# Six buffers of high parts, low parts in place, and GpSimd for every sixth low part of the light items

## The reference

```
hid = silu(tokens @ w1) * (tokens @ w3)      # 1024 x 3584 each
y   = gate * (hid @ w2)                      # 3584 x 1024
```

## Time and profile before

| | us |
|---|---|
| median of three runs (2112.20 to 2115.09) | 2114.43 |
| the profiled execution | 2117.29 |
| its span, first to last instruction | 2115.2 |
| first item, about | 1155.2 to 1282.8 |
| light items | 1282.8 to 1627.3 (114.8, 114.9, 114.8) |
| full items | 1627.3 to 2104.7 (119.6, 119.5, 119.6, ...) |

### The profile page before, as it was taken

How to read it: one execution, slowest core, us unless ns; L and a number is a source line. 1 busy time by engine, 2 the same in 40 slices (tenths; PEclk the granted TensorE clock), 3 DMA queues, 4 the chain that set the end, 5 groups by cost and what they waited for, 6 DMA issues and landing times.

```text
span 2115.2 us, 32333 instructions
## 1 busy us (share of the span) xinstructions
PE 2045.8 (97%) x12532; PEld 1762.9 (83%) x12532; DVE 1607.6 (76%) x1966; ACT 1303.7 (62%) x1611; POOL 80.5 (4%) x58
## 2 busy tenths in 40 slices
PE   6999999999999999999999999999999999999998
PEld 6899999999999989999999785555556888888886
DVE  6667986558885765555644888898888888888897
ACT  2645553555553654334643678888887777777776
POOL 0000000000000300000000000000000000000010
PEclk6999999999999999999999999999999999999999
DMA  9975455565445434554529899999999999999991
GB/s 288 242 236 173 154 167 140 134 185 185 121 140 152 148 109 148 182 188 132 184 66 355 325 370 382 404 388 395 388 406 377 383 374 384 376 379 386 358 396 72
DMA packets 315525, 548.27 MB, mean 259 GB/s; under 512 B 68364, under 2 KB 208577, under 8 KB 315401
## 3 DMA queue, kind: packets, MB, share of 16 engines
q1 hardware_dynamic: 306384, 530.81, 71.8%
q0 software_dynamic: 3168, 11.54, 1.8%
q10 hardware_dynamic: 5848, 4.19, 0.7%
HBM read 539.14 MB, written 7.36 MB: 258 GB/s over the span
## 4 chain that ended last, share of the span: by engine, by line
PE 85%; DVE 10%; ACT 3%; issue 1%; ACTq 0%; DMA 0%; DVEq 0%
PE bank L742 22%; PE bank L744 22%; PE bank L743 22%; DVE w_lo L2902 6%; PE bank L689 2%; PE bank L895 2%; PE bank L1325 1%; PE bank L1431 1%; PE bank L702 1%; ACT w_hi L2099 1%; PE bank L1432 1%; PE bank L727 1%; PE bank L1451 1%; PE bank L878 1%; PE bank L864 1%
## 5 line engine op out<-in xcount | busy, mean ns | idle before, releaser
L2902 DVE TENSOR_TENSOR w_lo<-pool,w_hi 128x2048 fp32r<-128x2048 f32 x336 | 761.3, 2288 | 87.9 <-ACT w_hi L2099 86.5
L2099 ACT ACTIVATE w_hi<-pool 128x2048 fp32r<-128x2048 f32 x336 | 638.5, 1915 | 133.8 <-PE bank L744 114.5
L742 PE MATMUL bank<-h_upper,upper 128*128 128x256 f32 x1056 | 312.0, 295 | 3.6 <-DVE h_lo L2439 3.2
L743 PE MATMUL bank<-h_lo,upper 128*128 128x256 f32 x1056 | 299.6, 284 | 0.0
L744 PE MATMUL bank<-h_upper,ring_lo 128*128 128x256 f32 x1056 | 299.5, 284 | 0.0
L2340 DVE TENSOR_TENSOR ring_lo<-ring,upper 128x1024 fp32r<-128x1024 f32 x148 | 179.9, 1221 | 102.9 <-ACT upper L1617 102.4
L742 PE MATMUL bank<-w_hi,xe_hi 128*128 128x512 f32 x560 | 222.5, 397 | 4.5 <-DVE w_lo L2902 4.5
L2639 DVE TENSOR_TENSOR piece_lo<-ring,piece_hi 128x1024 fp32r<-128x1024 f32 x118 | 145.0, 1237 | 97.3 <-ACT piece_hi L1606 97.0
L744 PE MATMUL bank<-w_hi,xe_lo 128*128 128x512 f32 x560 | 218.9, 391 | 0.0
L743 PE MATMUL bank<-w_lo,xe_hi 128*128 128x512 f32 x560 | 218.7, 391 | 0.0
L742 PEld LDWEIGHTS bank<-h_upper,upper 128*128 128x128 f32 x1056 | 203.0, 192 | 6.4 <-issue 4.7
(11 more groups left out here) (454 smaller groups left out, 3682.6 us busy)
## 6 DMA issues: line engine op xcount, KB each, us to landing
pool<-in_od_exp_w SPq DMA_DIRECT2D x336, 1024.0 KB, 7.9
ring<-in_w_in SPq DMA_DIRECT2D x48, 1024.0 KB, 5.4
ring<-in_ev_ffn_w SPq DMA_DIRECT2D x33, 1024.0 KB, 5.3
ring<-in_w_ada SPq DMA_DIRECT2D x24, 1024.0 KB, 6.5
ring<-in_od_w_in SPq DMA_DIRECT2D x12, 1024.0 KB, 5.9
ring<-in_ev_w_in SPq DMA_DIRECT2D x10, 1024.0 KB, 5.3
ring<-in_w_in SPq DMA_DIRECT2D x32, 256.0 KB, 4.6
ring<-in_w_out SPq DMA_DIRECT2D x8, 1024.0 KB, 5.0
```

The costliest lines, as they stand in the source:

```text
L742: nc.tensor.matmul(b, left[0], right[0], start=first, stop=False, skip_group_check=True)
L743: nc.tensor.matmul(b, left[0], right[1], start=False, stop=False, skip_group_check=True)
L2099: nc.scalar.activation(w_hi[q % 3], ring_slot(q), ACT.Copy)\
L2902: V.tensor_tensor(w_lo[q % 3], ring_slot(q), w_hi[q % 3].bitcast(F32), ALU.subtract)\
```

## The change

Three `w_hi`/`w_lo` pairs become six `w_hi`, and the low part is written over the half tile in its ring slot (`low_slot`). So SP may load q + 14 only once the product of q is done. ACT may run six half tiles ahead of PE. `BEHIND` and `LOW_ROWS` are moved back by one to three half tiles, the folds of w1 behind the second half tile that follows, and the folds of w3 behind both half tiles of `down`. In the light items the low parts of q = 3, 9, 15, 21, 27, 33 and 39 are formed by GpSimd, from a list written out for the three items, with `add_rows` ahead of q = 9 and `gather_rows` ahead of q = 27; PE waits for them on a semaphore of their own, and DVE counts such a step together with its next low part. `item_tables` is cut in three and done behind q = 7, 9 and 11, and PE's transposes of the gates wait for the gates alone.

```
@@ -159,6 +159,8 @@
...
         oa_hi = sb("oa_hi", 4, S, dt=F32R, within=over)
+    with ExitStack() as over:
+        expert_lo = [sb(f"expert_lo{n}", EHALF, dt=F32R, within=over) for n in range(ERING)]
     pool = ctx.enter_context(nc.sbuf_tensor("pool", [P, POOL], F32))[:, :]
@@ -194,9 +196,10 @@
...
-    w_hi, w_lo = [None] * 3, [None] * 3
-    for i in (1, 2, 0):
-        w_hi[i], w_lo[i] = sb(f"w_hi{i}", EHALF, dt=F32R), sb(f"w_lo{i}", EHALF, dt=F32R)
+    HIS = 6
+    w_hi = [None] * HIS
+    for i in (2, 3, 4, 5, 0, 1):
+        w_hi[i] = sb(f"w_hi{i}", EHALF, dt=F32R)
     xe_hi, xe_lo = sb("xe_hi", KD, P, dt=F32R), sb("xe_lo", KD, P, dt=F32R)
@@ -620,12 +624,16 @@
...
-    BEHIND = {1: [("y", 0)], 3: [("own rows", 0)], 5: [("hid", 0)], 9: [("hT", 0)], 11: [("gateT", 0)],
-              13: [("hid", 1), ("hid", 2)], 14: [("pick", 0)], 15: [("hT", 1)], 19: [("hT", 2)], 20: [("rows", 0)],
-              23: [("hid", 3), ("hid", 4)], 27: [("hT", 3)], 31: [("hT", 4)], 35: [("hid", 5), ("hid", 6)],
-              37: [("hT", 5)], 39: [("hT", 6)], 40: [("xe", 0)], 41: [("xe", 1)]}
-
-    LOW_ROWS = {3: (1, 0), 5: (3, 0), 9: (1, 1), 13: (3, 1), 19: (1, 2), 23: (3, 2), 31: (1, 3), 35: (3, 3)}
+    def low_slot(q):
+        return expert_lo[(q + ERING_FIRST) % ERING]
+
+    BEHIND = {4: [("y", 0)], 5: [("own rows", 0)], 7: [("hid", 0)], 11: [("hT", 0)], 13: [("gateT", 0)],
+              15: [("hid", 1), ("hid", 2)], 16: [("pick", 0)], 17: [("hT", 1)], 21: [("hT", 2)], 22: [("rows", 0)],
+              25: [("hid", 3), ("hid", 4)], 29: [("hT", 3)], 33: [("hT", 4)], 37: [("hid", 5), ("hid", 6)],
+              38: [("hT", 5)], 40: [("hT", 6)], 41: [("xe", 0), ("xe", 1)]}
+
+    LOW_ROWS = {4: (1, 0), 6: (3, 0), 10: (1, 1), 14: (3, 1), 20: (1, 2), 24: (3, 2), 32: (1, 3), 36: (3, 3)}
+    POOL_LOWERS = range(3, NH, 6)
     FIRST, LIGHTS = -1 - LIGHT, range(-LIGHT, 0)
@@ -1409,8 +1417,11 @@
...
-                pe.wait_ge(item_vector, at(item_vector, i, "lo", q))
-                return [split(w[q % 3], a, EHALF // a) for w in (w_hi, w_lo)]
+                if light and q in POOL_LOWERS:
+                    pe.wait_ge(pool_lower, when(pool_lower, i, q))
+                else:
+                    pe.wait_ge(item_vector, at(item_vector, i, "lo", q))
+                return [split(w, a, EHALF // a) for w in (w_hi[q % HIS], low_slot(q))]
@@ -1452,7 +1463,7 @@
...
-            def down(blk, behind=lambda: None):
+            def down(blk):
                 pe.wait_ge(item_vector, at(item_vector, i, "hT", blk))
@@ -1467,8 +1478,6 @@
...
                     m.then_inc(item_products, tick(item_products, "half", q))
-                    if half == 0:
-                        behind()
@@ -1478,29 +1487,30 @@
...
                 list_rows().then_inc(psum_ready, wrote("own rows"))
-            up(3, 0, 0)
+            up(3, 0, 0, 1)
             fold(1, 0)
-            up(3, 0, 1)
             if first:
...
                         pe.wait_ge(tok_ready, when(tok_ready, "x", t, g))
-            up(1, 1, 0)
+            up(1, 1, 0, 1)
             fold(3, 0)
-            up(1, 1, 1, 2, 3)
+            up(1, 1, 2, 3)
             turn_hidden(0)
             up(3, 1, 0)
-            fold(1, 1)
             if first:
                 pe.wait_ge(route_ready, when(route_ready, "own rows"))
-                pe.wait_ge(route_ready, when(route_ready, "tables"))
+                pe.wait_ge(route_ready, when(route_ready, "gates"))
             for t in range(NT):
...
             m.then_inc(item_products, tick(item_products, "gateT"))
-            up(3, 1, 1, 2, 3)
+            up(3, 1, 1)
+            fold(1, 1)
+            up(3, 1, 2, 3)
             if not first:
                 pe.wait_ge(item_scalar, at(item_scalar, i, "y", 1))
-            down(0, lambda: fold(3, 1))
+            down(0)
+            fold(3, 1)
             turn_hidden(1)
@@ -1509,20 +1519,22 @@
...
             list_rows().then_inc(item_products, tick(item_products, "rows"))
-            up(3, 2, 0)
+            up(3, 2, 0, 1)
             fold(1, 2)
-            up(3, 2, 1, 2, 3)
-            down(1, lambda: fold(3, 2))
+            up(3, 2, 2, 3)
+            down(1)
+            fold(3, 2)
             down(2)
...
             turn_hidden(4)
-            up(3, 3, 0)
+            up(3, 3, 0, 1)
             fold(1, 3)
-            up(3, 3, 1, 2, 3)
-            down(3, lambda: fold(3, 3))
+            up(3, 3, 2, 3)
+            down(3)
+            fold(3, 3)
             wait_turned(4)
@@ -2096,15 +2108,15 @@
...
                 act.wait_ge(s, value)
-            nc.scalar.activation(w_hi[q % 3], ring_slot(q), ACT.Copy)\
+            nc.scalar.activation(w_hi[q % HIS], ring_slot(q), ACT.Copy)\
                 .then_inc(item_scalar, tick(item_scalar, "hi", q) + more)
...
             if k == 3:
-                piece_of_expert(FIRST, 0, (piece_ready, when(piece_ready, piece_no[("gg3",), 1])), freed_at[where["odout", 0]])
+                piece_of_expert(FIRST, 0, (piece_ready, when(piece_ready, piece_no[("gg3",), 1])))
             if k == 5:
-                piece_of_expert(FIRST, 1, freed_at[where["odout", 2]])
+                piece_of_expert(FIRST, 1, freed_at[where["odout", 0]])
@@ -2148,11 +2160,11 @@
...
             for q, (w, blk, half) in enumerate(halves):
-                if first and q == 2:
-                    piece_of_expert(i, q, freed_at[where["router",]], more=2)
-                elif q > 2 or not first:
-                    piece_of_expert(i, q, (item_products, at(item_products, i, "half", q - 3) if q >= 3 else
-                                           at(item_products, i, "half", q - 3 + NH, items=-1)))
+                if first and 2 <= q < HIS:
+                    piece_of_expert(i, q, freed_at[where[("odout", q - 1) if q < HIS - 1 else ("router",)]], more=2 * (q == HIS - 1))
+                elif q > 1 or not first:
+                    piece_of_expert(i, q, (item_products, at(item_products, i, "half", q - HIS) if q >= HIS else
+                                           at(item_products, i, "half", q - HIS + NH, items=-1)))
                 if first and q == 17:
@@ -2899,7 +2911,7 @@
...
             dve.wait_ge(item_scalar, at(item_scalar, i, "hi", q))
-            V.tensor_tensor(w_lo[q % 3], ring_slot(q), w_hi[q % 3].bitcast(F32), ALU.subtract)\
+            V.tensor_tensor(low_slot(q), ring_slot(q), w_hi[q % HIS].bitcast(F32), ALU.subtract)\
                 .then_inc(item_vector, tick(item_vector, "lo", q) + more)
@@ -2983,6 +2995,7 @@
...
             V.tensor_copy(item_expert[:, 0:NE].bitcast(I32), item_order)
+            yield
             link(V.tensor_tensor(ours, iota8.unsqueeze(1).broadcast_to(square), item_order.unsqueeze(2).broadcast_to(square),
@@ -3026,6 +3040,10 @@
...
             ticks.counts[("route_ready", "items")] = ticks.counts["route_ready"]
+            yield
+
+        tables = item_tables()
+
@@ -3052,10 +3070,12 @@
...
             for q, (w, blk, half) in enumerate(halves):
-                if q > 1 or not first:
-                    expert_lower(i, q)
-                if first and q == 4:
-                    item_tables()
+                if light and q in POOL_LOWERS:
+                    tick(item_vector, "lo", q)
+                elif q > 1 or not first:
+                    expert_lower(i, q, more=int(light and q - 1 in POOL_LOWERS))
+                if first and q in (7, 9, 11):
+                    next(tables)
                 for step, n in after(q):
@@ -3195,9 +3215,18 @@
...
         gather_rows(-1)
+        for i in range(LIGHT):
+            for q in POOL_LOWERS:
+                if q == POOL_LOWERS[1]:
+                    add_rows(i)
+                if q == POOL_LOWERS[4]:
+                    gather_rows(i)
+                pool_engine.wait_ge(item_scalar, at(item_scalar, i - LIGHT, "hi", q))
+                G.tensor_tensor(low_slot(q), ring_slot(q), w_hi[q % HIS].bitcast(F32), ALU.subtract)\
+                    .then_inc(pool_lower, tick(pool_lower, i - LIGHT, q))
         pool_engine.wait_ge(route_ready, when(route_ready, "items"))
         count = pool_engine.value_load(item_count[0:1, 0:1].bitcast(I32), min_val=NE, max_val=MAXI)
-        with pool_engine.Fori(0, count - 1) as i:
+        with pool_engine.Fori(LIGHT, count - 1) as i:
             add_rows(i)
@@ -3241,7 +3270,7 @@
...
         for q in range(NH - ERING):
-            sp.wait_ge(item_vector, at(item_vector, FIRST, "lo", q))
+            sp.wait_ge(item_products, at(item_products, FIRST, "half", q))
             load(0, q + ERING)
@@ -3251,22 +3280,22 @@
...
         for q in range(NH - ERING, NH):
-            sp.wait_ge(item_vector, at(item_vector, FIRST, "lo", q))
+            sp.wait_ge(item_products, at(item_products, FIRST, "half", q))
             load(following, q + ERING - NH)
...
-                sp.wait_ge(item_vector, at(item_vector, i, "lo", q, items=-LIGHT))
```

(6 more changed lines are left out.)

## The result

The changed kernel takes 2142.97 us (median of four runs, 2132.65 to 2147.24), against 2114.76 for the kernel before beside it: ratio 1.0129, interval 1.0092 to 1.0166. It is 1.3% slower, and outside the predicted range. The profiled execution is the shortest of the four, 2132.65, so it shows only 15.4 us of the loss (span 2130.6, against 2115.2).

What follows compares the result with a forecast made beforehand. PE was taken to bound full items, and nothing alone light items, with their mutual waits. 2117.29 - 6.0 (tables) + 4.1 (three light items) = 2115.4, less 2.9 for the profiled execution's excess over the median: 2112.5 us; range 2101 to 2121.

Steps and rivals of the forecast that it cites:

- Does it run beside DVE?: Low parts on GpSimd and DVE: they take turns by whole instructions; seven moved ones take 31.5 us of turns, not 15.5.
- A light item, step by step: Light item laid out from its product 0: 116.2 us against 114.9 before, 1.4 more in each of three, +4.1 in all.
- my list (9, 17, 21, 26, 33): Five places in a light item where GpSimd's turns were to take back the gain of six buffers.
- What six buffers bring: Light items: fewer waits on low parts, taken back by GpSimd's turns; together 1.4 us more an item.
- The DMA ... can't become less than 110.2: Light item's 114.9 us at 393 GB/s: 410 at best allows 110.2, except ring stock, 2.6 us once per half tile.
- The tables in three parts: First item: PE's 4.50 us hole and lower clock go, 6.2 us together; 0.2 comes back at low part 12; -6.0.
- Rival 4: First item: the tables' third part makes the hole again at product 12; gain about 2.5, sum 2116; chance 0.07.
- The price of an undisturbed low part, 4.5: GpSimd's low part: 4.5 us, twice the 2.26 us of a half-length `tensor_tensor` with two different operands.
- Rival 1: GpSimd's low part costs 3.8 us; light items 112.6, total 2101.7; chance 0.32 with what lies between it and the forecast.
- Full items at 0: Four full items: no change from 119.5 us, as every low part stays two or more half tiles ahead.
- rival 2: GpSimd's turn is dearer, 5.2 us at each of five places in a light item; total 2123.1; chance 0.20.
- Rival 3: No turns taken at this length: DVE's load falls to 87 us, light items to 110.2 or 109; total 2090.7; chance 0.05.

Runs made afterwards that it cites:

- after: The changed kernel as profiled, all parts of the change against the kernel before; its profiled execution took 2132.65 us, the median of four runs 2142.97.
- experiment 2: Changed kernel with the next item's gather issued behind GpSimd's low part of q = 27 instead of ahead of it; 2140.78 us, ratio 1.0123.
- experiment 5: Changed kernel with GpSimd forming only the low part of q = 27 in each light item, DVE the other 41; 2123.75 us, ratio 1.0054.
- experiment 6: Changed kernel with GpSimd forming only the low part of q = 28 in each light item, DVE all others; 2116.38 us, ratio 1.0018.
- experiment 1: Changed kernel with all low parts of the light items on DVE, none on GpSimd; 2085.54 us, ratio 0.9867.
- experiment 3: Changed kernel with low part 27 given back to DVE, GpSimd keeping 3, 9, 15, 21, 33 and 39; 2103.5 us, ratio 0.9953.
- Experiment 9: Changed kernel, but in light items DVE waits for GpSimd's low part 27 before forming its own 28; 2113.47 us, ratio 0.9996.
- experiment 8: Changed kernel with GpSimd's seven low parts an item replaced by a memset of the same size; 2084.34 us, ratio 0.9868.
- experiment 4: Kernel before with only the tables cut in three, behind q = 6, 8 and 10, and gate transposes waiting for gates alone; 2112.39 us, ratio 0.9995.
- experiment 10: Changed kernel with GpSimd's low parts at three other places in each light item, such as 3, 18, 30; 2111.73 us in one execution.

## Why the prediction was wrong

**The failed step is "Does it run beside DVE? ... So they take turns, whole instruction by whole instruction."** The first half held: the two didn't run at the same time. A low part of DVE that began while GpSimd had its turn ended 2.1 us after GpSimd's did (at q = 21 of after's first light item 1335.14 against 1333.00, recorded with 4.53). The second half assumed fair turns, one instruction each. With the next low part ready each time, DVE kept the turn, for 12 to 14 us in after's first light item and in every one of experiments 2, 5 and 6, and for nearly 7 in after's other two. That is 39 of the 57 us that GpSimd's work costs (experiments 1, 3). The rows I drew it from had only short queues: in the earlier trace rows DVE itself waited for high parts between its low parts (1.66 and 0.19), so GpSimd found gaps. I read a rule for a full queue from a stretch without one.

**"A light item, step by step" came out right for fair turns, in sum.** It gave 116.2, with product 27 not late. Experiment 9, where the turn at 27 is enforced, has 115.6 and 116.6 between gathers. In its second light item PE waited for GpSimd at 9, 21 and 33, as laid out (1.46, 1.87 and 1.90 us). At 26, where the layout had 1.9 us, it didn't wait, and a wait of 1.56 at product 2 wasn't in the layout, so part of the agreement is luck. In after the items lose another 3 to 10 us, at product 27, where my list (9, 17, 21, 26, 33) had 1.9 us for low part 26 and nothing for 27.

**What six buffers bring was never priced by itself.** It stood in the layout only as netted against GpSimd's turns (+1.4). By itself the rest of the change brings 28 us (experiment 1), 23 of it over the three light items. Had I laid out the item with all low parts on DVE, the comparison would have shown that every us of the gain was there without GpSimd, and the question would have been what GpSimd adds: with free relief, nothing (experiment 8).

**"The DMA ... can't become less than 110.2"** is undercut: 105.9. The stated exception, what the ring holds in advance, was priced at 2.6 a half tile once. The steady rate was a little higher (403 over a whole item), and the rest is stock: loads landing in 19.5 us tell that it runs low. An estimate from the stretches: 403 GB/s over 105.9 us are 42.7 MB, where 393 over 114.9 were 45.2, so an item took some 2.5 MB from the ring's stock, worth about 6 us at that rate. By this estimate a longer row of light items would not stay at 105.9; no run shows it.

**"The tables in three parts", -6.0, measured about -3.3** (first item, from its first product to the transposes of the next tokens, 111.5 against 114.8, the same in after and experiment 1). Product 12 was 1.35 us late, not 0.2, and the transposes of `turn_hidden(1)` 1.62, which I had counted in light items only:

```profile
1189.33 0.47 PE L750 MATMUL bank<-w_hi,hT_hi 128*128 128x512 f32 x1 [1.35 <-DVE expert_lo L2914]
...
1196.64 0.66 PE L1462 MATMUL bank<-ident,hid 128*128 128x128 f32 x4 [1.62 <-DVE hid L3089]
```

These are after's two waits of PE behind low parts and `hid` there. Rival 4 had named product 12. With three buffers, and the parts one half tile earlier, the longest wait is twice that, at product 11 (2.71, experiment 4).

**The price of an undisturbed low part, 4.5, was right:** 4.59 to 4.63. Rival 1's 3.8 is refuted.

**Full items at 0** held: 119.2 against 119.5, PE without a wait.

**The rivals.** The nearest in sign was rival 2, "GpSimd's turn is dearer", at 2123. Its mechanism, a dearer instruction at every place, isn't what happened: six of seven cost 4.6 to 6.3, and one cost 11 to 18. But one of its grounds was "turns lost to DVE", and that is what was lost, at one place. I had written that handing over costs nothing as an argument against it, and from one row. Rival 3 (no turns, 2090.7) came within 5.2 us of what the change gives without GpSimd's low parts (2085.5), by the wrong cause.

Why low part 27 took 11.3 us in the second and third item and 18.5 in the first, and 18.5 three times in experiment 2, can be read from the traces: in the 11.3 high part 30 came 0.52 us after low part 29 had ended, in the 18.5 it was ready 0.26 us or more before. A shift of under a us so decides over 7 us. The runs of after spread by 14.6 us, and the profiled one is the shortest; two items by 7.2 us more would be 14.4, but only that one has a trace, so that this is the spread's cause isn't shown. What stays open is why GpSimd gets the turn at q = 3 of two items though DVE's next low part is ready, and what 128x1 instructions have that lets them in (below).

## What to carry to other kernels

Before work is moved to a second engine that shares a path with a busy one, ask how long the busy one's queue of ready instructions is at that moment: the newcomer may be served only when that queue is empty. More buffers allow a longer queue; here six let six low parts go first, and GpSimd's low parts with fewer buffers were not run. Price each part of a change alone as well as in sum, since here a gain of 28 us stood beside a loss of 57 and was netted away on paper. And ask what the relieved engine was worth: when a third resource stands close behind, removing its work brings nothing.

## What the runs showed of the hardware

- Two-operand subtractions on DVE, each ready when the one before ends, can keep a GpSimd subtraction waiting for all of them: up to 18.8 us for a 4.6 us instruction, behind six of DVE's. Wherever it was passed over, 61 times in seven traces, DVE's next operand was ready (experiment 10). The Trainium skill (SBUF — State Buffer, "Who interferes with whom") says that issue order decides who blocks. Here the measurement differs: GpSimd's instruction began at 1342.99 and DVE's low parts at 1343.49 and later, and all six of these went first. When each engine asks for the ports isn't recorded, so the first of the six could be a matter of half a us; the last three began 7.4 us later and more.
- Tiny instructions of GpSimd (128x1) do get in, at the end of the one low part in progress: 2.17 us at 1335.86 of after, with the next low part following at once, instead of 0.19 at 1151.37.
- A 128x2048 float32 memset on GpSimd takes 1.81 us and slows no subtraction of DVE (experiment 8).
- Loads of 1 MB ran at 403 GB/s over 212 us (experiment 1), their median from issue to landing 19.5 us instead of 8.1 in its second half.
